# Quarter products of gate and up: three 256-column products into half a bank, two bank sets, five reads

## The reference

```python
def swiglu(h, w_gu, w_down):
    g, u = jnp.split(h @ w_gu, 2, axis=-1)
    return (jax.nn.silu(g) * u) @ w_down
...
    hf = rmsnorm(x, norm_ffn_g[l])
    x = x + swiglu(hf, w_gu[l], w_down[l])
return rmsnorm(x, final_norm_g)
```

## Time and profile before

| what | value |
|---|---|
| median of three runs | 2745.27 us (2743.96 to 2745.40) |
| profiled execution: span | 2743.1 us; the median of the runs is 2.2 us above it, for what lies around the span |
| TensorE busy | 2704.5 us, 99% |
| VectorE busy | 1737.1 us, 63% |
| ScalarE busy | 1017.7 us, 37% |
| GpSimd busy | 766.3 us, 28% |
| data moved | 333.29 MB, 121 GB/s |

### The profile page before, as it was taken

One profiled execution on the slowest core, in us unless ns is written; L12 is line 12 of the kernel. 1 busy time (PEld: TensorE's weight loads), 2 busy tenths in 40 slices (PEclk: granted clock), 3 DMA queues, 4 the chain that ended last, 5 costly groups with the idle time before them and its releaser, 6 DMA issues.

```text
span 2743.1 us, 34950 instructions
## 1 busy us (share of the span) xinstructions
PE 2704.5 (99%) x13710; PEld 2279.2 (83%) x13710; DVE 1737.1 (63%) x1820; ACT 1017.7 (37%) x1134; POOL 766.3 (28%) x642
## 2 busy tenths in 40 slices
PE   9999999999999999999999999999999999999997
PEld 7888888888778888888788888888888888888886
DVE  6677652334653344573677767687777777777786
ACT  6555432224642232243553333333333332222224
POOL 0000000000000003330357666776667632212120
PEclk9999999999999999999999999999999999999999
DMA  6221233322222325333434444434343463444432
GB/s 239 77 85 62 83 97 99 92 84 92 77 93 92 99 77 207 93 121 109 139 109 137 132 138 132 138 101 146 127 143 127 143 238 123 161 146 137 161 125 82
DMA packets 125889, 333.29 MB, mean 121 GB/s; under 512 B 10320, under 2 KB 57424, under 8 KB 125136
## 3 DMA queue, kind: packets, MB, share of 16 engines
q1 hardware_dynamic: 119296, 309.37, 35.3%
q10 hardware_dynamic: 6480, 22.35, 2.0%
HBM read 301.27 MB, written 30.41 MB: 121 GB/s over the span
## 4 chain that ended last, share of the span: by engine, by line
PE 92%; DVE 4%; ACT 1%; DMA 1%; issue 1%; SPq 0%; DVEq 0%; ACTq 0%
PE ps L2198 16%; PE acc L1812 14%; PE acc L1814 14%; PE acc L1813 14%; PE ps L2201 8%; PE acc L1832 6%; PE acc L1834 6%; PE acc L1833 6%; PE acc L2198 3%; PE acc L2201 1%; DMA x_tokens<-x_n 1%; PE ps L1874 1%; PE ps L1863 1%; DVE w_lo L1588 1%; ACT ps L799 0%
## 5 line engine op out<-in xcount | busy, mean ns | idle before, releaser
L1101 DVE TENSOR_TENSOR w_lo<-raw,w_hi 128x1024 fp32r<-128x1024 f32 x328 | 475.9, 1456 | 274.9 <-ACT w_hi L609 274.3
L1812 PE MATMUL acc<-act_both,w_hi 128*128 128x512 f32 (+1 forms) x1536 | 591.1, 385 | 3.6 <-DVE w_lo L1101 3.1
L1814 PE MATMUL acc<-act_both,w_lo 128*128 128x512 f32 (+1 forms) x1536 | 585.3, 381 | 0.0
L1813 PE MATMUL acc<-act_both,w_hi 128*128 128x512 f32 (+1 forms) x1536 | 584.9, 381 | 0.0
L609 ACT ACTIVATE w_hi<-raw 128x1024 fp32r<-128x1024 f32 x328 | 344.3, 1055 | 553.9 <-PE acc L1814 340.7
L1812 PEld LDWEIGHTS acc<-act_both,w_hi 128*128 128x128 f32 x1536 | 289.6, 189 | 59.4 <-DVE w_lo L1101 3.7
L1814 PEld LDWEIGHTS acc<-act_both,w_lo 128*128 128x128 f32 x1536 | 289.5, 188 | 55.4
L1813 PEld LDWEIGHTS acc<-act_both,w_hi 128*128 128x128 f32 x1536 | 289.8, 189 | 54.3 <-issue 0.7
L543 POOL MEMSET mem_stat<- 128x256 f32 x1 | 0.3, 312 | 1047.1 <-DMA mem<-mem_t 1047.1
L2198 PE MATMUL ps<-t_both,w_hi 128*128 128x512 f32 x896 | 281.6, 396 | 0.5 <-DVE cg L1616 0.5
L1832 PE MATMUL acc<-act_both,w_hi 128*128 128x512 f32 x672 | 262.9, 391 | 3.1 <-DVE x L1456 3.0
(11 more groups left out here) (306 smaller groups left out, 4752.8 us busy)
## 6 DMA issues: line engine op xcount, KB each, us to landing
raw<-w_stream SPq DMA_DIRECT2D x412, 512.0 KB, 3.6
over<-w_stream SPq DMA_DIRECT2D x84, 512.0 KB, 4.4
gate_t<-cg ACTq DMA_DIRECT2D x22, 512.0 KB, 2.6
over<-gate_t SPq DMA_DIRECT2D x22, 512.0 KB, 5.3
up_t<-cu ACTq DMA_DIRECT2D x20, 512.0 KB, 2.6
over<-up_t SPq DMA_DIRECT2D x20, 512.0 KB, 6.2
x<-x_t SPq DMA_DIRECT2D x16, 512.0 KB, 8.6
x_tokens<-x_n SPq DMA_DIRECT2D x4, 1024.0 KB, 15.4
```

The source lines that it names most:

```text
L1101: nc.vector.tensor_tensor(w_lo[:, s, :], raw[:, s, :], f(w_hi[:, s, :]), ALU.subtract)\
L1812: nc.tensor.matmul(dst, wh, ah, start=start and k == 0, stop=False)
L1813: nc.tensor.matmul(dst, wh, al, start=False, stop=False)
L1814: last = nc.tensor.matmul(dst, wl, ah, start=False, stop=stop and k == UK - 1)
```

## The change

It changes how a product of this stage is accumulated, where it lies, and how it is read.

- A product is three matmuls of 256 columns for each j, all into one half bank: hi weights by high activations, hi by low, lo by high.
- A group takes four of the eight banks: products 0 and 1 in the first, 2 and 3 in the second, and so on. Groups alternate between the two sets. Only the first matmul into a bank has `start`.
- TensorE waits at a group's first unit for the reading of the group two before; for group 0 it waits for the last direct copy (`A_DOWN`).
- VectorE reads a group in five operations once all four units are done, and tells it once.
- The stores wait for a whole reading, and the down projection's first outputs for that of the group before the last.

```diff
-READ_STEPS = 3
-FREED_BY = {1: 1, 3: 2, 5: 3}
-TOLD = (0, 2, 4)
...
-        acc = [ctx.enter_context(nc.psum_tensor(f"acc{n}", [P, S], F32)) for n in range(2)]
-        both_ps = ctx.enter_context(nc.psum_tensor("ps", [P, 6 * S], F32))
-        ps = [both_ps[:, 3 * S * n:3 * S * (n + 1)] for n in range(2)]
+        banks = ctx.enter_context(nc.psum_tensor("banks", [P, 8 * S], F32))
+        acc = [banks[:, S * n:S * (n + 1)] for n in range(2)]
+        ps = [banks[:, 2 * S + 3 * S * n:2 * S + 3 * S * (n + 1)] for n in range(2)]
...
-                    act.wait_ge(products_read, READ_STEPS * (2 * p - 1))
+                    act.wait_ge(products_read, 2 * p - 1)
...
+        def half_bank(bank_set, i):
+            at = 4 * S * bank_set + SH * i
+            return banks[:, at:at + SH]
+
+        def two_products(bank_set, i):
+            at = 4 * S * bank_set + SH * i
+            return banks[:, at:at + 2 * SH].rearrange("p (a s) -> p a s", a=2)
...
-                n = g % 2
+                b = g % 2
...
                 both_tiles = [P, 2, SH]
-                dve.wait_ge(products_done, len(TOLD) * g + 1)
-                link(nc.vector.tensor_copy(out[:, 1, :], half(0, 1)))
-                link(nc.vector.tensor_tensor(out[:, 1, :], half(0, 0), out[:, 1, :], ALU.add))
-                dve.wait_ge(products_done, len(TOLD) * g + 2)
-                added(out[:, 0:4:3, :], out[:, 1:2, :].broadcast_to(both_tiles), lambda h: two_banks(0, h), freed)
-                dve.wait_ge(products_done, len(TOLD) * g + 3)
-                added(out[:, 1:3, :], out[:, 3:4, :].broadcast_to(both_tiles), lambda h: two_banks(1, h))
-                added(out[:, 3, :], out[:, 2, :], lambda h: half(3, h), freed)
+                dve.wait_ge(unit_done, U_MIX + 4 * (g + 1))
+                link(nc.vector.tensor_copy(out[:, 1, :], half_bank(b, 0)))
+                link(nc.vector.tensor_tensor(out[:, 0:4:3, :], two_products(b, 1),
+                                             out[:, 1:2, :].broadcast_to(both_tiles), ALU.add))
+                link(nc.vector.tensor_tensor(out[:, 1:3, :], two_products(b, 3),
+                                             out[:, 3:4, :].broadcast_to(both_tiles), ALU.add))
+                link(nc.vector.tensor_tensor(out[:, 3, :], half_bank(b, 3), out[:, 2, :], ALU.add))
+                nc.vector.tensor_tensor(out[:, 1:3, :], two_products(b, 5), out[:, 1:3, :], ALU.add)\
+                    .then_inc(products_read, 1)
+                dve.wait_ge(products_read, g + 1)
                 between()
-                dve.wait_ge(unit_done, U_MIX + 4 * (g + 1))
-                added(out[:, 1:3, :], out[:, 1:3, :], lambda h: two_banks(2, h), freed)
...
-                    dst = bank(g % 2, at)
-                    if c == 0 and g and at in FREED_BY:
-                        pe.wait_ge(products_read, READ_STEPS * (g - 1) + FREED_BY[at])
+                    dst = half_bank(g % 2, at)
                     src = act_both if kind == "b" else t_both
                     for j in range(2):
-                        nc.tensor.matmul(dst, hi[:, w_block, P * j:P * (j + 1)], src[:, :, ks.start + 2 * c + j, toks],
-                                         start=c == 0 and j == 0, stop=False)
-                    for j in range(2):
-                        last = nc.tensor.matmul(dst[:, SH:S], lo[:, w_block, P * j:P * (j + 1)],
-                                                src[:, 1, ks.start + 2 * c + j, toks], start=False,
-                                                stop=c == 3 and j == 1)
-                    if c == 3 and at in TOLD:
-                        last.then_inc(products_done, 1)
+                        k = ks.start + 2 * c + j
+                        wh, wl = (t[:, w_block, P * j:P * (j + 1)] for t in (hi, lo))
+                        nc.tensor.matmul(dst, wh, src[:, 1, k, toks], start=c == 0 and j == 0 and at % 2 == 0, stop=False)
+                        nc.tensor.matmul(dst, wh, src[:, 0, k, toks], start=False, stop=False)
+                        last = nc.tensor.matmul(dst, wl, src[:, 1, k, toks], start=False,
+                                                stop=c == 3 and j == 1 and (at % 2 == 1 or at == len(PRODUCTS) - 1))
...
-                    if g < 2:
-                        pe.wait_ge(acc_free, A_DOWN - 1 + g)
+                    if g == 0:
+                        pe.wait_ge(acc_free, A_DOWN)
+                    elif g > 1:
+                        pe.wait_ge(products_read, g - 1)
...
-            down(0, split.at(), banks=(READ_STEPS * (2 * MIXES - 2) + 1, READ_STEPS * (2 * MIXES - 1) + 1))
+            down(0, split.at(), banks=(2 * MIXES - 1, 2 * MIXES - 1))
```

More of the change, by code:

```diff
@@ L314, in block_kernel @@
         gated, hid_made, products_read = sem("gated"), sem("hid_made"), sem("products_read")
-        products_done = sem("products_done")
         gate_t = nc.dram_tensor("gate_t", (FFN // P // 2, P, 2, S), F32).ap()
@@ L1035, in _ @@
                 else:
-                    act.wait_ge(products_read, READ_STEPS * 2 * p)
+                    act.wait_ge(products_read, 2 * p)
                     store_up(p)
@@ L1629, in read_products @@
-                added(out[:, 1:3, :], out[:, 1:3, :], lambda h: two_banks(2, h), freed)
-            read = Tally()
             both = rstd[:].unsqueeze(1).broadcast_to([P, 2, S])
```

## The result

The changed kernel takes 2787.5 us (median of four, 2786.7 to 2788.2) against 2745.3 before (four runs): a ratio of 1.0153, 95% interval 1.0138 to 1.0167. It is slower by 1.5%, and 2788 was forecast.

What follows compares the result with a forecast made beforehand. TensorE, 99% busy at full clock, bounds the kernel. Matmuls 846.7 + boundary 21.3 + start 1.7 + GpSimd 2 = 871.7 us against the stage's 829.3, +42.4, giving 2788 us; range for 8 in 10, 2766 to 2806.

Steps and rivals of the forecast that it cites:

- The matmuls: Stage's 1176 products, six 256-column matmuls each at 0.1200 us: 846.7 us, +28.6; other bound about nothing.
- The boundary: After G, next group's first matmul, reading then split delay TensorE's second unit: 0.52 us at 41 boundaries, 21.3 us.
- the slow restart: At unit two after a split, TensorE's first pair of matmuls takes 0.10 us longer, 0.72 or 0.73 for 0.63.
- The start: Group 0 waits for ScalarE's last direct copy, starting at about 1411.65 instead of 1409.93: +1.7 us, once.
- Collisions with GpSimd: Boundaries where VectorE's split meets GpSimd's sums, as in 8 of 41 before: 2 us added.
- that rival: VectorE's split collides with GpSimd's sums at the boundaries, 0.88 x 41 = +36 us: 2824; chance 0.13.
- Behind the stage: Down projection's first outputs and first addition expected to cost nothing; cover 0.2 us, some tenths if gone.
- 11.2 of old waits: Small TensorE waits in the stage before the change, beyond 818.1 us of products; included in the subtraction.
- The product and boundary bounds: Forecast's own range, 2778 to 2798: product 0.718 to 0.722 us, boundary 0.4 to 0.7 us.
- The time without a wait at the boundary: Rival: reading or split quicker by 0.4 us, so the boundary's 21.3 us fall away: 2766; chance 0.08.
- The narrow matmuls at the rate of their columns: Rival: 256 columns take 0.107 us in the stage, some 27 us shorter: 2718; chance 0.04.
- TensorE's instruction supply: Rival: 7056 matmuls for 4704 strain supply; mean spacing 0.125 us gives +26 us: 2814; chance 0.03.

Runs made afterwards that it cites:

- e2: The changed kernel with the split for the next group's second unit made before the reading instead of after it: 2764.8 us, ratio 1.0072.
- e3: The changed kernel with reading begun inside the last unit, only the last of five operations after the group's end: 2764.6 us, ratio 1.0068.
- e4: The changed kernel with the first reading operation of each group done three times instead of once: 2822.4 us.
- e6: The kernel of e2 with each lo by hi matmul of 256 columns made in two of 128: 3006.9 us.
- e1: The kernel before with only each wide 512-column matmul made in two of 256, banks and reading unchanged: 2766.7 us, ratio 1.0074.

## Why the prediction was right, point by point

**The matmuls: +28.6, right.** The spacing of 0.1200 from the 48 matmuls of the earlier trace rows held for all 7056. e2 and e3 isolate it: 846.8 us between the first and the last. The other bound, 0.115 from single starts inside a product, did not come true. The 109 ns of the Trainium skill (TensorE: Matmul & The Clock Gate, Back-to-back issue gap) is that page's gap of an isolated matmul; of a stream with weight loads it says that both set the spacing, so it was the wrong figure to set against this stage, as a forecast or as a rival. The trace has 120 in e2 and e3 throughout.

**The boundary: 0.52 x 41 = 21.3, right, and a little large.** Each time that made it up was met: reading at G + 0.27, split over at G + 5.39 for 5.38, unit two at G + 5.45 for 5.46, period 20.66 for 20.68. From the first matmul to the end of the stage are 868.1 us, 21.4 above the matmuls' 846.7, and 0.7 of these are slower splits (below), so 20.7 are left. For the slow restart the prediction named 0.72 or 0.73 for a pair; its rows have 0.72 and 0.69. The changed kernel shows the 0.10 that was put in. e2 and e3 take the wait away, e4 makes it larger one for one.

**The start: 1.7, right.** 1410.09 to 1411.73 is 1.64.

**Collisions with GpSimd: 2 us put in, mis-sized.** The splits after the 41 readings last 2.02 or 2.03 but for four of 2.15 to 2.23, 0.7 us in all. GpSimd's burst ends 1.7 us after G, at 1661.10, and the split starts at 1662.75:

```profile
1660.36 0.74 POOL L569 TENSOR_TENSOR raw<-raw 128x256 f32<-128x256 f32 x1
1668.23 1.01 POOL L566 TENSOR_TENSOR raw<-raw 128x256 f32<-128x256 f32 x1 [7.13 <-DMA raw<-w_stream]
```

The gap is 1.65 us where it was 0.3, as the argument against that rival had it. In e3, where the split starts 1.9 us sooner, the two do meet at most boundaries, and the split takes some 0.45 us longer, half of the 0.88 that the rival had put in.

**Behind the stage: put at nothing, not told apart from scatter.** From the stage's end to the end of the span are 505.4 us, 503.9 before. The waits of the down projection for VectorE's additions are 5.0 us against 3.2 in the whole run. But this stretch, which the edits touch at its beginning at most, takes anything from 503.5 (e6) to 506.3 (e1) in the profiles of the experiments, and in e3, with the new layout, it takes 503.9 again. One profile of each doesn't show that the 1.5 us belong to the change. So part of the closeness of the total (2787.5 for 2788) is luck: the stage came out 1.9 us below its sum, mostly for the 1.3 us too much for GpSimd, and what lies behind it 1.5 us above.

**The ranges.** The product and boundary bounds of the prediction give 2781 to 2798; its 2778 is reached only with the 2 us for GpSimd taken off as well. The 2.2 us between span and median are not all time around the span: where a profiled execution's own time is on record, it is 1.7 to 1.8 above its span (2787.0 for 2785.2 in the changed kernel). The rest is that the median run is a little longer than the profiled one.

**The rivals.** The time without a wait at the boundary was put at 2766; e2 and e3, which have none, are at 2765, so its price was right and it did not happen. The narrow matmuls at the rate of their columns, the case for faster, falls by e1. TensorE's instruction supply kept up: 846.78 us for 7056 matmuls leaves no room for a stall.

**Where the loss is.** Of the stage's +40.5: matmuls 28.6, boundary 21.4 (the 0.7 of slower splits included), start 1.6, less the 11.2 of old waits; the boundary is what the others leave, and e2 and e3 measure it at 21.3. The new layout with its waits repaired (e3, 848.3 us for the stage, its start counted as above) is no better than the old one with the same narrow matmuls (e1, 848.9). No version here beats the kernel before, whose wide matmuls are worth more than all its waits.

## What to carry to other kernels

Price a matmul by the distance between starts in a long undisturbed run of the very shape, and look for that shape elsewhere in the same kernel. Splitting a 512-column matmul into two of 256 cost 12 to 13 ns each time here, with everything else hidden (28.6 us for 2352 of them). Going on to 128 columns cost 103 ns for each matmul added (e6).

Saving work on an engine with idle time helps only if the saved work stands between two things that wait for each other. Write the loop down (group's end, reading, next conversion, remaining units): ten operations of which eight can start early are shorter, in that loop, than five that all start late. If there is a second set of buffers, use it for that order as well: do what the other engine needs next before emptying the buffer that nobody waits for.

## What the runs showed of the hardware that was not expected

A matmul of 128 columns, with its own weight load, is hardly cheaper than one of 256. With 512, 256 and a mixture of 256 and 128 columns the spacing is 0.227, 0.120 and a mean of 0.1157 us at full clock. The first two fit the columns at 2.4 GHz and 13 ns beside them; by that the mixture would have a mean of 0.093. The Trainium skill (TensorE: Matmul & The Clock Gate, LDWEIGHTS (loading the stationary operand)) gives a load as its columns over 1.2, an estimated 107 ns for 128; the mean of 116 ns in e6 is somewhat more. The even starts of the loads in e6 speak for them as the limit, but it was not isolated: every matmul of this stage carries a load, and no run has narrow matmuls without one.

VectorE's split of a unit took 2.03 us where GpSimd was idle (1662.75 in the changed kernel) and 2.48 where it overlapped the last of GpSimd's sums (1675.19 in e3). No edit moved GpSimd's sums alone, so their part in it is read from the traces and not tested.
